# Value projections of the mLSTM, the GLA, the NSA and the dilated attention computed in pairs with the tokens on the rows, and no longer transposed

## The reference

```python
# block 1
h = rmsnorm(x, g)
q_m, k_m, v_m, if_pre, o_pre, q_a, k_a, v_a, gate_pre = split(h @ w_in)
hm  = mlstm_cell(silu(conv(q_m)), silu(conv(k_m)), v_m, ...)         # 4 heads of 256
for g, (window, dilation) in enumerate(((128, 1), (512, 4), (2048, 16))):
    o_g, lse_g = dilated_window_attention(q_a[g], k_a[g], v_a[g])    # 3 groups of 8 heads of 64
y_b = sum(softmax(lses) * outs)
x = x + (sigmoid * (y_a @ w_proj_a) + sigmoid * (y_b @ w_proj_b)) @ w_out;  x = x + ffn(rmsnorm(x))
# block 2
h = rms_norm(x)
o_gla = gla_mixer(g_q, g_k, g_v, ...)                                # 4 heads, values of 256
o_nsa = nsa_mixer(n_q, n_kc, n_vc, n_ks, n_vs, n_kw, n_vw, ...)      # 8 heads of 64
x = x + rms_norm(mixed @ w_out);  x = x + rms_norm(ffn(rms_norm(x)))
```

## Time and profile before

| | |
|---|---|
| median of 3 runs | 1910.94 us (1910.94 to 1911.08) |
| span of the profiled execution, first to last instruction | 1909.1 us |
| difference to the median, outside the span | 1.8 us |
| PE busy | 1898.5 us, 99% |
| DVE busy | 1255.4 us, 66% |
| ACT busy | 735.3 us, 39% |
| granted TensorE clock | 1.000 over the whole span |

### The profile page before, as it was taken

The page is one execution under the profiler, slowest core; times in us unless marked ns, Lnnn a source line. Parts: engine busy times, 40 slices in busy tenths (PEclk is TensorE's granted clock), DMA queues, the critical chain, the costliest instruction groups (busy, mean ns, idle before and its releaser), DMA issues.

```text
span 1909.1 us, 26308 instructions
## 1 busy us (share of the span) xinstructions
PE 1898.5 (99%) x10599; PEld 1591.0 (83%) x10599; DVE 1255.4 (66%) x1894; ACT 735.3 (39%) x1265; POOL 265.1 (14%) x156
## 2 busy tenths in 40 slices
PE   9999999999999999999999999999999999999998
PEld 7788888888888888999997778877777878899998
DVE  7777543345455748777776756766776667887874
ACT  6332322233334444344435522224444354444442
POOL 0211210111111113000004001121111133100002
PEclk9999999999999999999999999999999999999999
DMA  5322233232321323233333222322121322333332
GB/s 177 102 70 85 88 86 115 89 99 67 89 67 45 115 91 104 78 106 102 114 108 103 77 67 78 100 79 65 56 67 40 116 79 87 100 100 100 100 130 81
DMA packets 53472, 172.77 MB, mean 90 GB/s; under 512 B 5963, under 2 KB 10643, under 8 KB 53352
## 3 DMA queue, kind: packets, MB, share of 16 engines
q1 hardware_dynamic: 52912, 170.66, 28.8%
q10 hardware_dynamic: 440, 0.44, 0.1%
HBM read 168.86 MB, written 2.22 MB: 90 GB/s over the span
## 4 chain that ended last, share of the span: by engine, by line
PE 94%; DVE 3%; ACT 1%; POOL 1%; issue 0%; DVEq 0%
PE PS L1561 22%; PE PS L1563 22%; PE PS L1562 22%; PE PS L1637 5%; PE PS L1639 5%; PE PS L1638 5%; PE PS L1983 1%; PE PS L2005 1%; PE PS L1780 1%; PE PS L1795 1%; PE PS L1961 1%; PE PS L1841 1%; PE PS L1827 1%; PE PS L1818 1%; PE PS L1748 1%; POOL XT L3338 1%
## 5 line engine op out<-in xcount | busy, mean ns | idle before, releaser
L1561 PE MATMUL PS<-HH,WH 128*128 128x512 f32 x1124 | 444.0, 395 | 0.8 <-DVE WL L2467 0.7
L1563 PE MATMUL PS<-HH,WL 128*128 128x512 f32 x1124 | 438.0, 390 | 0.0
L1562 PE MATMUL PS<-HL,WH 128*128 128x512 f32 x1124 | 437.4, 389 | 0.0
L2064 ACT ACTIVATE WH<-RAW 128x1024 fp32r<-128x1024 f32 (+2 forms) x256 | 261.1, 1020 | 336.4 <-PE PS L1563 271.4
L2467 DVE TENSOR_TENSOR WL<-RAW,WH 128x1024 fp32r<-128x1024 f32 (+2 forms) x195 | 251.2, 1289 | 113.7 <-ACT WH L2064 112.0
L1561 PE MATMUL PS<-AH,WH 128*128 128x512 f32 x816 | 323.7, 397 | 0.0
L1563 PE MATMUL PS<-AH,WL 128*128 128x512 f32 x816 | 318.1, 390 | 0.0
L1562 PE MATMUL PS<-AL,WH 128*128 128x512 f32 x816 | 317.6, 389 | 0.0
L1561 PEld LDWEIGHTS PS<-HH,WH 128*128 128x128 f32 x1124 | 211.1, 188 | 49.7 <-issue 4.2
L1563 PEld LDWEIGHTS PS<-HH,WL 128*128 128x128 f32 x1124 | 211.0, 188 | 45.1
L1562 PEld LDWEIGHTS PS<-HL,WH 128*128 128x128 f32 x1124 | 211.2, 188 | 42.2 <-issue 0.2
(11 more groups left out here) (360 smaller groups left out, 2260.7 us busy)
## 6 DMA issues: line engine op xcount, KB each, us to landing
RAW<-wst SPq DMA_DIRECT2D x292, 512.0 KB, 3.6
RAW<-wst SPq DMA_DIRECT2D x16, 256.0 KB, 2.6
RAW<-wst SPq DMA_DIRECT2D x8, 384.0 KB, 3.1
XT<-xT SPq DMA_DIRECT2D x3, 512.0 KB, 7.3
out<-XT SPq DMA_DIRECT2D x4, 384.0 KB, 2.5
AR<-mx SPq DMA_DIRECT2D x4, 256.0 KB, 6.2
AR<-scr SPq DMA_DIRECT2D x16, 64.0 KB, 4.3
AR<-scr SPq DMA_DIRECT2D x8, 128.0 KB, 4.8
```

Source lines behind the costliest of these rows:

```text
L1561: T.matmul(out, wh, XH[:, k, :], start=k == 0, stop=False)
L1562: T.matmul(out, wh, XL[:, k, :], start=False, stop=False)
L1563: m = T.matmul(out, wl, XH[:, k, :], start=False, stop=k == nk - 1)
L2064: t = A.activation(whole(WH, i, n), raw(i)[:, 0:n], ACT.Copy, scale=1.0)
```

## The change

Eleven pairs of units are formed: `vm` (2,3), (4,5), (6,7); `gv` (2,3), (4,5), (6,7); `vs` with `vw`; and for each pair of heads hp `va` 4+hp with `va` 8+hp. In a pair the operands swap places. A block of 128 tokens of the activations stands in the array, and 256 features (both units' 128) of the weights stream past it. The result has the tokens on the partitions at once. The weights in memory are repacked: the pair's first unit has rows 0 to 511 of both features' blocks, its second rows 512 to 1023, so each unit still has 1024 values in a row to load and to split. Each unit does its half of the rows for all four blocks of tokens; token blocks 0 and 1 are summed in the first unit's bank, 2 and 3 in the second's. So both banks stay in use until the second unit runs.

```diff
+def token_pairs():
+    pairs = [[(n, 2 * h), (n, 2 * h + 1)] for n in ("vm", "gv") for h in (1, 2, 3)] + [[("vs", 0), ("vw", 0)]]
+    pairs += [[("va", 4 + hp), ("va", 8 + hp)] for hp in range(4)]
+    return {AT[x + (0,)]: (AT[a + (0,)], AT[b + (0,)]) for a, b in pairs for x in (a, b)}
...
     def pair(hp):
-        for g in range(3):
-            for n in ("qa", "ka", "va"):
-                add(n, 4 * g + hp)
+        for n, g in (("qa", 0), ("ka", 0), ("va", 0), ("qa", 1), ("ka", 1), ("qa", 2), ("ka", 2), ("va", 1), ("va", 2)):
+            add(n, 4 * g + hp)
...
+        def token_block(X, k, i, t):
+            if UNITS[i][0] == "va":
+                return X[:, k, t:512:4]
+            return X[:, k, 128 * t:128 * t + 128]
...
+            def token_products(s, i, steps):
+                XH, XL, x = moving(UNITS[i][0], 0)
+                first, second = TOKEN_PAIRS[i]
+                for n in steps:
+                    t_, r = n // 2, n % 2
+                    u = (first, second)[t_ // 2]
+                    out = PS[:, s.bank["sum", u], t_ % 2 * 256:t_ % 2 * 256 + 256]
+                    if i == first and n % 4 == 0:
+                        s.free("sum", u)
...
+                    for k in (2 * r, 2 * r + 1):
+                        wh, wl = whole(WH, i, 1024)[:, 256 * k:256 * k + 256], whole(WL, i, 1024)[:, 256 * k:256 * k + 256]
+                        kx = k + 4 * (i == second)
+                        xh, xl = token_block(XH, kx, i, t_), token_block(XL, kx, i, t_)
+                        T.matmul(out, xh, wh, start=kx == 0 and t_ % 2 == 0, stop=False)
+                        T.matmul(out, xh, wl, start=False, stop=False)
+                        m = T.matmul(out, xl, wh, start=False, stop=kx == 7 and t_ % 2 == 1)
...
+            def tokens_out(s, i, x):
...
+                for n in (0, 1):
+                    t_ = 2 * x + n
+                    dst, src = token_place(i, t_), PS[:, b, 256 * n:256 * n + 256]
+                    t = V.tensor_scalar(dst, src, FT[:, o + t_:o + t_ + 1], None, ALU.mult, ALU.bypass)
```

More of the change, by code:

```diff
@@ L306 @@
     pair_products = pair_keep = pair_held = pair_add = pair_silu = pair_hi = pair_lo = none
+    token_factors = tokens_out = none
     chunk_add = chunk_hi = chunk_lo = forms_x = forms = forms_hi = forms_lo = none
@@ L422, in ahead, with sums_of @@
         e.load(i + 5)
+def sums_of(e, i):
+    pair = TOKEN_PAIRS.get(i, (i,))
+    if i == pair[0]:
+        for x in pair:
+            e.sum_bank("sum", x)
 def quarter(e, i, q):
@@ L427, in quarter @@
         ahead(e, i)
-        e.sum_bank("sum", i)
+        sums_of(e, i)
     e.products(i, range(2 * q, 2 * q + 2))
+    if q == 1 and i in TOKEN_PAIRS and i == TOKEN_PAIRS[i][1]:
+        e.tokens_out(i, 0)
     if q % 2:
@@ L434, in evict @@
 def evict(e, i):
+    if i in TOKEN_PAIRS:
+        if i == TOKEN_PAIRS[i][1]:
+            e.tokens_out(i, 1)
+        return
     e.evict(i)
@@ L642, in mlstm @@
     e.gate_columns()
+    e.turn_bank("factors", "n1")
+    e.token_factors("n1")
     e.load_max((3,))
@@ L928, in gla @@
     e.log_sigmoids((0, 1))
+    e.turn_bank("factors", "n3")
+    e.token_factors("n3")
     quarter(e, i, 0)
@@ L940, in gla @@
     for n, j in GLA_FIRST[4:]:
+        if (n, j) == GLA_FIRST[-1]:
+            e.ring = [0, 1]
         unit(e, unit_of(n, j))
@@ L1155, in build @@
         RC = sb("RC", [128, 16])
+        FT = sb("FT", [128, 8])
         reached = {}
@@ L1549, in free, with token_factors @@
                     pe.wait_ge(*at("free", *s.before[key]))
+            def token_factors(s, norm):
+                b = s.bank["factors", norm]
+                s.free("factors", norm)
+                pe.wait_ge(*at("con"))
+                pe.wait_ge(*at("free", "spread", norm))
+                for q in range(4):
+                    t = T.transpose(PS[:, b, q * 128:(q + 1) * 128], RB[:, q * 128:(q + 1) * 128], ident())
+                t.then_inc(*pe_done["norm"].next("factors_turned", norm))
+            def token_products(s, i, steps):
[7 more added lines that the diff above has]
+                        s.free("sum", u)
+                    if n == 0:
+                        pe.wait_ge(*at("lo", i))
+                    for k in (2 * r, 2 * r + 1):
+                        wh, wl = whole(WH, i, 1024)[:, 256 * k:256 * k + 256], whole(WL, i, 1024)[:, 256 * k:256 * k + 256]
+                        kx = k + 4 * (i == second)
+                        pe.wait_ge(*at(x, "lo", kx))
+                        xh, xl = token_block(XH, kx, i, t_), token_block(XL, kx, i, t_)
+                        T.matmul(out, xh, wh, start=kx == 0 and t_ % 2 == 0, stop=False)
+                        T.matmul(out, xh, wl, start=False, stop=False)
+                        m = T.matmul(out, xl, wh, start=False, stop=kx == 7 and t_ % 2 == 1)
+                    if i == second and n == 3:
+                        m.then_inc(*unit_sum.next("half", i))
+                    elif n == 7:
+                        m.then_inc(*unit_sum.next("unit", i))
             def products(s, i, ks):
+                if i in TOKEN_PAIRS:
+                    return s.token_products(i, ks)
                 name, j, k0, nk = UNITS[i]
@@ L2776, in after, with token_factors @@
                     s.kept(i, name, j)
+            def token_factors(s, norm):
+                dve.wait_ge(*at("factors_turned", norm))
+                o = 0 if norm == "n1" else 4
+                t = V.tensor_copy(FT[:, o:o + 4], PS[:, s.bank["factors", norm], 0:512:128])
+                t.then_inc(*dve_done["norm"].next("free", "factors", norm))
+            def tokens_out(s, i, x):
+                u = TOKEN_PAIRS[i][x]
+                name, j = UNITS[i][:2]
+                norm = norm_of(name)
+                o, b = 0 if norm == "n1" else 4, s.bank["sum", u]
+                dve.wait_ge(*at("free", "factors", norm))
+                if name == "va":
+                    s.slot_free(j % 4)
+                elif name == "vm" and j > 3:
+                    dve.wait_ge(*at("summed", j // 2 - 2, 3))
+                elif name == "gv" and j > 3:
+                    dve.wait_ge(*at("across", j // 2 - 2, 1))
+                dve.wait_ge(*(at("unit", i) if x else at("half", i)))
+                for n in (0, 1):
+                    t_ = 2 * x + n
+                    dst, src = token_place(i, t_), PS[:, b, 256 * n:256 * n + 256]
+                    if len(dst.shape) > 2:
+                        src = src.rearrange("p (x c) -> p x c", x=2)
+                    t = V.tensor_scalar(dst, src, FT[:, o + t_:o + t_ + 1], None, ALU.mult, ALU.bypass)
+                t.then_inc(*bank_read.next("free", "sum", u))
+                if x:
+                    for u in TOKEN_PAIRS[i]:
+                        bank_read.named("free", "tokens", u)
             def kept(s, i, name, j):
@@ L3466, in pack_units @@
             continue
+        if i in TOKEN_PAIRS:
+            k = 512 * TOKEN_PAIRS[i].index(i)
+            both = [m[order[x][0]][k:k + 512, order[x][1] * 128:order[x][1] * 128 + 128] for x in TOKEN_PAIRS[i]]
+            w[i] = np.concatenate(both, axis=1).reshape(4, 128, 256).transpose(1, 0, 2).reshape(128, 1024)
+            continue
         blk = m[name][k0 * 128:(k0 + nk) * 128, j * 128:(j + 1) * 128]
```

10 lines of the change are left out of this document (added).

## The result

| | before | after |
|---|---|---|
| median of 5 runs each | 1910.94 us (1910.92 to 1911.08) | 1954.34 us (1954.20 to 1954.45) |
| span of the profiled execution | 1909.1 us | 1952.2 us |
| PE busy | 1898.5 us | 1940.1 us |
| DVE busy | 1255.4 us | 1239.0 us |

The change makes the kernel slower: 1.0227 times the time before, 95% interval 1.0215 to 1.0238. The forecast was 1947.0 us with a range up to 1953. So the direction and the largest term's mechanism held, but the time is 7.3 us above the forecast and 1.3 us above the range.

What follows compares the result with a forecast made beforehand. PE's own work was taken to bound the kernel. Transposes -9.9, reshaped products +4.2, factors +0.6 and stepped loads +41 gave +36 us on 1910.94, so 1947 us, range 1905 to 1953.

Steps and rivals of the forecast that it cites:

- stepped load: Attention's four va pairs: 384 loads in steps of 16 bytes no longer hide, 0.107 us more each, 41 us.
- reshaped products: All 11 pairs: 48 products of 512 columns become 96 of 256 at 0.1175 us, 4.2 us more.
- DVE's cover: At va pairs, DVE evicts banks in time because it mostly waits for PE; taken as 0, at worst 2 us.
- transposes, factors, waits: Across stages: 88 transposes removed, 9.9 us less; two added factor groups, 0.6 us more; bank waits taken as 0.
- What bounds the kernel: Whole kernel: PE's own work sets the time, 1898.5 of 1909.1 us busy; a faster DVE alone buys nothing.
- two DVE rows: DVE's stepped read and write cost 1.75 and 1.84 ns a value, used as upper price of PE's va loads.
- Twice the contiguous 0.115: Va pairs: a stepped load of 128 values takes double a contiguous one, 0.230 us, supporting the upper price.
- Transposes and factors: GLA, mLSTM, attention: removed transposes save 4.6, 2.6 and 2.6 us; factor groups add 0.46 and 0.1, given as 0.6.
- The step is free: Rival for the va loads: stepping costs PE nothing, sum -5.1 us, 1905.8 us; chance 0.25.
- partly slowed: Rival for the va loads: pitch 0.14 to 0.19 us, 9 to 28 us less 5.1, 1915 to 1934 us; chance 0.08.
- Free, but the gain is lost: Rival: free step, but bank waits of two us and pitch 0.119 us for 1056 products, 1909.4 us; chance 0.12.
- only 2 ns to spare: Contiguous load of 0.115 us just hides beneath a 256-column product of 0.1175, so even a tenth of the step's cost shows.

Runs made afterwards that it cites:

- E7: Changed kernel with contiguous standing blocks in the va pairs and the streamed weight columns read in steps of 4 values instead; 1954.67 us, ratio 1.0229.
- E3: Changed kernel with the va standing blocks read in steps of 2 values instead of 4; 1911.23 us, ratio 1.0001 to the kernel before.
- E4: Changed kernel with the va standing blocks read in steps of 3 values instead of 4; 1932.54 us, ratio 1.0113 to the kernel before.
- E10: Kernel before plus the seven non-va pairs, weight split moved behind the first bank's eviction in each gv pair's second unit; 1910.33 us, ratio 0.9997.
- E2: Changed kernel without the va pairs and with the attention units' old order, seven other pairs kept; 1911.86 us, ratio 1.0005 to the kernel before.
- E1: Changed kernel with the va standing blocks as 128 neighbouring tokens instead of every fourth; 1911.18 us, ratio 1.0001 to the kernel before.
- E8: Kernel before with standing weights of 24 qa and ka units read in steps of 4 beneath 512-column products; 1917.15 us, ratio 1.0032.

## Why the prediction was wrong in its size and right in its mechanism

The steps that failed are three sizes in the sum, all to the same side: the stepped load was put at 41 us and took 43.1; the reshaped products were put at 4.2 us, by a price read from products with weights standing, and took 6.8; and DVE's cover was taken to hold at no cost, where waits that the change lengthens took about 2.5. The terms, by the two spans (+43.1 us; forecast +35.9, the part outside the span grew by 0.3):

| term | forecast | measured |
|---|---|---|
| stepped load, 384 | +41 | 384 x (0.2322 - 0.1199) = +43.1 |
| 528 products made 1056 | +4.2 | 1056 x 0.1199 - 528 x 0.227 = +6.8 |
| transposes, factors, waits | -9.3 | the rest, -6.8 |

- **What bounds the kernel.** Right: PE still has 94% of the chain, and DVE's 16.4 us less (10 to 15 forecast) bought nothing.
- **The stepped load.** The step that decides held. Of the two DVE rows I took the read's 1.75 ns a value; PE's is 1.81, between it and the write's 1.84. That is 2.1 us over 384 loads. That the two engines' prices a value are so near is in part luck: I took them for a time of the memory, "whichever way it goes", and PE's own stepped stream takes 0.91 ns a value (E7). "Twice the contiguous 0.115", 0.230, was within 1%, and its idea is the one that E7 bears out, but its number rests on a misreading (below the list). I also priced the step as a time by the value, and E3 and E4 show that a load's goes by the group of 16 bytes. At step 4 the two are the same, so the forecast didn't suffer; at step 2 mine would have been wrong by the whole term.
- **Products reshaped.** The assumption in the text failed: "a 256-column product with activations standing costs what one with weights standing does". It takes 0.1199 us and not 0.1175, so a pair costs 0.62 us more and not 0.38. I had the 0.119 in a rival, as a loss that comes only there, and it belonged into the sum. Worth 2.6 us. Why it is 2.4 ns slower is open; the loads' lengths, 192 against 188 ns, show it and don't explain it.
- **Transposes and factors.** The first factor group costs 0.49 us (scores of head 0 at 60.62 instead of 60.13; 0.46 forecast), and 88 transposes are gone, 48 remain. (The parts of the forecast's 9.9 us, 4.6, 2.6 and 2.6, add up to 9.8.) The second group moves the GLA's entry by 0.4 us, and the wait of 1.10 us that is gone gives it back, as forecast. Of the three stages that were to get shorter by 1 us or so each, the mLSTM did, by 0.8 us; GLA and NSA did not (0.05 us over both).
- **DVE and the banks.** "The cover holds" failed, mostly in the GLA's `gv` pairs and not where I looked. The two waits cost 1.4 us from start to start, and E10 without them is 1.5 us below E2. The wait at L2074 is 0.3 us longer: `vw`'s transposes had stood where PE waited in any case, so I counted a gain there that wasn't to be had. The second wait for a split is 0.3 us longer and the softmax's transposes take 0.4 us more; what causes these two wasn't looked at. Together that is 2.4 of the 2.5 us that the last row of the table is short.
- **The rivals.** "The step is free" is refuted by E1 beside the result, "partly slowed" (0.14 to 0.19) holds for step 3 and not for 4. "Free, but the gain is lost" described, without the step, what E1 and E2 showed in kind, a pitch near 0.119 us and waits for banks, and was still too low: 1909.4 against 1911.2 and 1911.9.
- **The range.** Its upper end was the upper price of the load, 45, plus 3 us for waits. By the text's own terms that is 1910.94 - 9.9 + 4.2 + 0.6 + 48 = 1953.8 us and not 1953, and the measured time is 0.5 us above that. It had no room for the second term's error, though a rival in the same text held it.

The misreading: in the earlier trace rows the 1.84 us reach from the first start to the modelled end of the last product, and are not what sixteen starts take. The next product starts here:

```profile
1547.09 0.68 PE L1545 MATMUL PS<-C 128*128 128x256 f32 x2
```

Sixteen products in 1547.09 - 1545.39 = 1.70 us are 0.106 us each and not 0.115. So a contiguous load had more than "only 2 ns to spare", and twice it is 0.21 us: that 0.230 came near the measured 0.232 was luck.

The gain expected of the plain pairs went the same way: seven pairs cost 7 x 0.62 = 4.3 us in narrower products and 0.5 or more in factors, and save 56 transposes in 14 groups, about 6 us by the earlier trace rows. The 1.5 us or so that this leaves was eaten by the two waits for banks, 1.4 us.

## What to carry to other kernels

Swapping the operands of a product to get rid of a transpose halves the columns that stream past each load; here the eight transposes of a pair were worth 0.9 us and its 48 more instructions cost 0.62, so that two short waits took what was left. Before letting an access pattern do a regrouping on PE, count the groups of 16 bytes that the standing block touches: with float32, half as many groups as values was free here; as many groups as values doubled the pitch of 256-column products and cost 5% under 512 columns. Price a wait by the distance between two starts and not by its bracket in the timeline: 0.44 us in the bracket cost 0.7. When an eviction is moved to the middle of a unit, read what stands ahead of it in its engine's queue at every place, the mixers' longest included.

## What was not expected of the hardware

- A stepped stream is slowed as well as a stepped load: 256 values in steps of 16 bytes take 0.233 us instead of 0.120 (E7), at 0.91 ns a value.
- A step of 2 float32 values costs nothing for a load: 195 ns against 192, pitch 0.1199 in both (E3, E1). A step of 8 costs 3% more pitch than a step of 4 (0.2402 against 0.2322), though both give one value for each 16 bytes.
- A load of 0.232 us costs 0.011 us beneath a product of 0.227 us (E8, by the pitch of the changed kernel): the longer of the two sets the pitch, with a few ns on top.
- Products with activations standing run at 0.1199 us where those with weights standing run at 0.1175, both contiguous. The cause is open.
